# Expert results stored at a row per token and rank instead of added in memory

## The chip, the cores and the metric

The kernel runs on one core of a Trainium2 chip. The metric is the device time of one execution in microseconds, lower is better; a kernel's time is the median of several runs.

## The reference

Two layers over 512 latent tokens and 256 context tokens of 1024 values, float32. A layer is a mixer (attention) and a mixture of experts, each added to the stream through a norm and a gate. The change touches the second half alone:

```python
# moe: t tokens, 64 experts, 8 of them for each token, one shared expert for all
scores = sigmoid(xt @ router_w)
...                                   # idx: the 8 experts of a token, wts: their weights
routed[tok] += (silu(xb @ w1[e]) * (xb @ w3[e])) @ w2[e] * slot_w      # for every block of an expert
shared = (silu(xt @ sw1) * (xt @ sw3)) @ sw2
return routed + shared
# layer: x += gate2 * RMSNorm_post(moe(...))
```

An expert has F = 256 hidden columns, so w1, w3 and w2 are 1 MB each. Layer 0 has 768 tokens, layer 1 has 512 (the context isn't wanted behind it): 6144 and 4096 pairs of token and expert.

## The kernel before

Phases follow each other with a barrier between them. Of a layer they are: `project` and the attention, `settle`, `experts`, `combine`.

`settle` ends the mixer, writes the modulated rows of all tokens to HBM (`h_rows`), routes them, and works out the shared expert, whose result SP stores tile by tile (128 tokens) to `y_rows` (L1060). Vector makes the mask of chosen experts (`r_maskb`, L1324) and a table for each token and expert in bf16: three parts of the weight and two parts of the token's number. GpSimd writes a block of zero rows to both tensors (L1071, L1072). TensorE is at work nearly all through it with the shared expert; the last shared result is taken out of PSUM by L1253.

`experts` runs over blocks of up to 128 tokens of one expert; an expert with more tokens has more blocks, and the last slots of a block can be empty. They point at spare rows behind the last token. Each engine has its own loop over blocks, two blocks a turn, held together by semaphores:

- SP loads w1 and w3 of an expert (two loads of 1024 KB) into one of two halves of `ring`, once Vector has split what was there. ACT issues the load of w2 (1024 KB, L1627).
- Vector makes the one-hot matrix `e_sel` (L1718); TensorE multiplies it with the table (`index`, L1536), which gives each slot's token and weight; Vector puts the token's number into `e_idxs` (L1728), five blocks ahead.
- GpSimd gathers the rows of a block (`gather`, copy L1486 and indirect DMA L1489) and adds a block's results to `y_rows` (`scatter`, copy L1496 and indirect DMA L1501). The order in its loop is gather of block b + 4, scatter of block b. The scatter's first wait is `added`, that the scatter before has landed, since an addition in memory reads its row and writes it later and two experts can have the same token. Both use queue 0.
- TensorE turns the gathered rows (L1545), multiplies them with the split weights (L1559, L1565), turns the gated product (L1574) and multiplies it with w2 (`down`, L1585). ACT casts the weights' high part (L1647) and takes the result out of PSUM times its weight into one of two buffers `e_y` (`rows_out`, L1673, once per block). Vector makes the low part of the weights (`e_w13l`, L1739, four pieces an expert, both inputs in SBUF).

`combine` loads the finished rows of each tile (L1802) and the gate's row for each condition (L1805; two conditions in layer 0, one in layer 1), ACT makes the norm's factor (L1824 to L1826), Vector updates the stream with two instructions a tile (L1849, L1851). In layer 0 ACT goes on to the next norm's sums (L1833 to L1839); in layer 1 SP stores the output (L1810).

```python
def scatter(b, par):
    wait_for(pool, added, 16 * b)
    nc.gpsimd.tensor_copy(sidx[par][:], idxs[:, at_block(b)]).then_inc(s_copied, 1)
    pool.wait_ge(y_ready, b + 1)
    pool.wait_ge(s_copied, b + 1)
    nc.gpsimd.indirect_dma_start(s.yrows[l], ..., ysb[par][:], None, compute_op=ALU.add).then_inc(added, 16)
```

Of the kernel before, what the change touches and what calls it, by code (L numbers as in the profile page):

```python
# [8 lines left out]
F32 = mybir.dt.float32  # L9
F32R = mybir.dt.float32r  # L10
BF16 = mybir.dt.bfloat16
# [6 lines left out]
P = 128  # L18
D = 1024
# [17 lines left out]
ROUTED_SCALE = 2.5  # L37
RING = 3
# [920 lines left out]
def settle(nc, s, a, l, tiles, r):  # L959
# [18 lines left out]
    with ExitStack() as ctx:  # L978
# [22 lines left out]
        maskb = sb("r_maskb", [P, n_t, E], BF16)  # L1001
        wsum, winv = sb("r_wsum", [P, n_t]), sb("r_winv", [P, n_t])
# [23 lines left out]
        zero_ready, ones_ready = sem("zero_ready"), sem("ones_ready")  # L1026
# [15 lines left out]
        def _(sp):  # L1042
# [24 lines left out]
        def _(pool):  # L1067
# [4 lines left out]
            pool.dma_start(s.yrows[l][T:T + P, :], zero[:]).then_inc(zero_out, 16)  # L1072
            pool.wait_ge(zero_out, 32)
# [182 lines left out]
        def _(dve):  # L1256
# [74 lines left out]
            link(nc.vector.tensor_copy(r.tab5[:, :, :, 0], wt[:]))  # L1331
            link(nc.vector.tensor_tensor(res1[:], wt[:], r.tab5[:, :, :, 0], ALU.subtract))
            link(nc.vector.tensor_copy(r.tab5[:, :, :, 1], res1[:]))
            link(nc.vector.tensor_tensor(res1[:], res1[:], r.tab5[:, :, :, 1], ALU.subtract))
            link(nc.vector.tensor_copy(r.tab5[:, :, :, 2], res1[:]))
            for i in range(n_t):
                link(nc.vector.memset(r.tab5[:, i, :, 3], float(i * P - T - P)))
            link(nc.vector.tensor_copy(r.tab5[:, :, :, 4], part[:, 0:1].unsqueeze(2).to_broadcast([P, n_t, E])))
# [60 lines left out]
def experts(nc, s, a, l, n_t, r):  # L1399
# [10 lines left out]
    with ExitStack() as ctx:  # L1410
# [7 lines left out]
        idxs, gws = sb("e_idxs", [P, P], U32), sb("e_gws", [P, P])  # L1418
# [9 lines left out]
        gathered = [sem(f"gathered{i}") for i in range(2)]  # L1428
        (w13_in, w2_in, w13_hi, w13_lo, sel_ready, idx_mm, tok_ready, idx_ready, g_copied, s_copied, xg_clean, xt_mm, x_hi,
         x_lo, h_mm, e_ready, g_ready, gt_mm, gt_ready, y_mm, y_ready, added, pool_clear, sp_clear, act_clear) = (sem(n) for n in (  # L1430
             "w13_in", "w2_in", "w13_hi", "w13_lo", "sel_ready", "idx_mm", "tok_ready", "idx_ready", "g_copied", "s_copied",
             "xg_clean", "xt_mm", "x_hi", "x_lo", "h_mm", "e_ready", "g_ready", "gt_mm", "gt_ready", "y_mm", "y_ready",
             "added", "pool_clear", "sp_clear", "act_clear"))
# [3 lines left out]
        raw2 = s.ring[:, 2, :].rearrange("p (o k n) -> p o k n", o=2, k=KF)  # L1437

# [41 lines left out]
        def _(pool):  # L1480
# [43 lines left out]
            pool.wait_ge(added, 16 * (2 * n + 1))  # L1524
# [4 lines left out]
        def _(pe):  # L1529
            def index(b, par, code):  # L1530
# [4 lines left out]
                for t in range(n_t):  # L1535
                    mm = nc.tensor.matmul(psI[:, 0:5], sel[par][:, t, :], r.tab5[:, t, bass.DynSlice(e, 1), :],  # L1536
# [87 lines left out]
        def _(act):  # L1624
# [50 lines left out]
            def step(b, par, code, later):  # L1675
# [4 lines left out]
                if not isinstance(b, int) or b > 0:  # L1680
                    rows_out(b - 1, 1 - par)
# [13 lines left out]
            step(0, 0, code[0], code[2])  # L1695
            step(1, 1, code[1], code[3])
            with act.Fori(0, n - 1) as i:
                code = codes(act, 2 * i + 2, 4)
                step(2 * i + 2, 0, code[0], code[2])
                step(2 * i + 3, 1, code[1], code[3])  # L1700
# [3 lines left out]
            rows_out(m + 1, 1)  # L1704
            next2(m + 2, code[0])
            gate(m + 2, 0)
            rows_out(m + 2, 0)
# [203 lines left out]
```

## Time and profile before

| | |
|---|---|
| median of 3 runs | 3057.51 us (3044.96 to 3065.29) |
| the profiled execution, and its span | 3069.55 us, 3067.8 us |
| TensorE busy | 87% of the span |
| Vector, ACT, GpSimd busy | 50%, 42%, 18% |
| mean granted clock of TensorE | 0.926 |
| moved by DMA | 645.89 MB |
| blocks of experts, layer 0 and layer 1 | 77 and 71 |
| expert stages, first to last result taken | 720.9 to 1592.9 us, 2226.7 to 3033.3 us |
| addition stages | 1607.6 to 1633.1 us, 3047.7 us to the end |

The span is the profile's own, from the first instruction to the last end; the time around it is some 2 us longer. The profiled execution is 12 us above the median of the three runs. Below, PE is TensorE, DVE is Vector, POOL is GpSimd, L12 is line 12 of the kernel before. Durations and times are in us unless they are marked ns. The expert stages are some 1700 of the 3068 us, the addition stages some 45.

### The profile page before, as it was taken

What the parts mean: (1) busy time and instruction counts of PE and PEld (TensorE: products, weight loads), DVE (VectorE), ACT (ScalarE), POOL (GpSimd) and SP (SyncE); (2) the same over time, 40 slices, a digit from 0 to 9 for tenths busy, and PEclk for the clock granted to TensorE, in tenths of its full rate; (3) what the DMA queues carried; (4) which work ended last, traced back from release to release, by engine and by line L of the source; (5) the groups of instructions that cost most, each with busy time, mean ns of one, the idle gap of its engine ahead of it and who ended that gap; (6) DMA issues with size and microseconds to landing.
All of it is one profiled execution on the core that took longest, in us unless ns stands there. A gap on an engine that the chain in (4) does not pass through costs nothing. (4 is left out here: it accounts for less than half of the span.)

```text
span 3067.8 us, 50203 instructions
## 1 busy us (share of the span) xinstructions
PE 2677.9 (87%) x11125; PEld 1635.2 (53%) x11126; DVE 1534.4 (50%) x2814; ACT 1303.4 (42%) x2063; POOL 561.2 (18%) x624
## 2 busy tenths in 40 slices
PE   5598999978889989999965999989698889989994
PEld 0044454535556666666642444654366666666663
DVE  0143663336555655565634212953555566665562
ACT  1022663215545545454533112642255555555562
POOL 0000000002222332333220000000123323333331
PEclk6699899998999999999987999989899999999997
DMA  9820202128998999798974101011488999999896
GB/s 400 343 74 3 56 1 74 69 97 314 307 292 273 330 313 305 239 323 262 300 194 162 71 11 58 1 41 69 158 296 285 322 311 328 335 319 341 248 328 169
DMA packets 135713, 645.89 MB, mean 211 GB/s; under 512 B 24024, under 2 KB 31192, under 8 KB 78936
## 3 DMA queue, kind: packets, MB, share of 16 engines
q1 hardware_dynamic: 72576, 383.49, 32.9%
q0 software_dynamic: 43200, 121.69, 18.1%
q10 hardware_dynamic: 19864, 139.80, 12.0%
q8 instruction: 39, 0.64, 0.1%
q14 instruction: 34, 0.28, 0.0%
HBM read 588.17 MB, written 92.37 MB: 222 GB/s over the span
## 5 line engine op out<-in xcount | busy, mean ns | idle before, releaser
L1559 PE MATMUL e_psH<-e_w13h,e_xh 128*128 x1184 | 611.6, 517 | 63.6 <-issue 32.3
L1739 DVE TENSOR_TENSOR e_w13l<-ring,e_w13h x512 | 592.7, 1219 | 113.0 <-ACT e_w13h L1647 109.7
L1585 PE MATMUL e_psY<-ring,e_gt 128*128 x1184 | 566.8, 606 | 6.6 <-ACT e_gt L1660 6.6
L1647 ACT CAST e_w13h<-ring x512 | 497.8, 1043 | 163.3 <-DMA ring<-in_exp_w 127.9
L1559 PE MATMUL e_psH<-e_w13l,e_xh 128*128 x1184 | 486.3, 411 | 0.0
L1752 DVE TENSOR_TENSOR e_xl<-e_psT,e_xh 128x512 fp32r<-128x512 f32 x296 | 197.5, 688 | 500.6 <-ACT e_xh L1667 377.5
L1545 PE MATMUL e_psT<-ident,e_xg 128*128 128x128 f32 x1184 | 335.3, 286 | 70.7 <-DMA e_xg<-h_rows,e_gidx 67.6
L459 PE MATMUL psP<-ring,ho 128*128 128x512 f32 x800 | 349.5, 592 | 0.0
L1559 PEld LDWEIGHTS e_psH<-e_w13h,e_xh 128*128 128x128 f32 x1184 | 235.9, 199 | 181.6 <-issue 147.4
L1565 PE MATMUL e_psH<-e_w13h,e_xl 128*128 x1184 | 307.9, 402 | 0.0
L1545 PEld LDWEIGHTS e_psT<-ident,e_xg 128*128 128x128 f32 x1184 | 227.2, 192 | 140.5 <-issue 78.4
L1585 PEld LDWEIGHTS e_psY<-ring,e_gt 128*128 128x128 f32 x1184 | 213.5, 190 | 166.0 <-issue 153.9
L1501 POOL DMA_INDIRECT y_rows<-e_y,e_sidx x148 | 249.0, 1682 | 191.9 <-ACT e_y L1673 89.7
L1667 ACT CAST e_xh<-e_psT 128x512 fp32r<-128x512 f32 x296 | 169.1, 588 | 261.8 <-PE e_psT L1545 156.2
L1559 PEld LDWEIGHTS e_psH<-e_w13l,e_xh 128*128 128x128 f32 x1184 | 237.5, 201 | 18.0 <-issue 17.5
L459 PEld LDWEIGHTS psP<-ring,ho 128*128 128x128 f32 x800 | 149.1, 190 | 173.6 <-issue 173.6
L1565 PEld LDWEIGHTS e_psH<-e_w13h,e_xl 128*128 128x128 f32 x1184 | 211.2, 188 | 43.0
L1496 POOL COPY e_sidx<-e_idxs 128x1 uint32 (+1 forms) x148 | 63.4, 428 | 824.3 <-DMA y_rows<-e_y,e_sidx 824.3
L1673 ACT ACTIVATE e_y<-e_psY,e_gws 128x1024 f32<-128x1024 f32 x148 | 164.1, 1109 | 95.1 <-PE e_psY L1585 73.5
L1489 POOL DMA_INDIRECT e_xg<-h_rows,e_gidx x148 | 166.8, 1127 | 126.5 <-POOL e_gidx L1486 125.6
L1718 DVE TENSOR_TENSOR e_sel<-slots,posm 128x768 bf16 (+1 forms) x156 | 128.9, 828 | 32.5 <-DMA slots<-in_k_slots 30.6
L1486 POOL COPY e_gidx<-e_idxs 128x1 uint32 (+1 forms) x148 | 119.4, 807 | 88.2 <-PE e_psT L1545 65.6
(252 smaller groups left out, 2594.5 us busy)
## 6 DMA issues: line engine op xcount, KB each, us to landing
ring<-in_exp_w SPq DMA_DIRECT2D x256, 1024.0 KB
ring<-in_exp_w ACTq DMA_DIRECT2D x130, 1024.0 KB
ring<-in_ada_w SPq DMA_DIRECT2D x48, 1024.0 KB, 13.3
ring<-in_c_w_in SPq DMA_DIRECT2D x6, 2048.0 KB
ring<-in_sh_w SPq DMA_DIRECT2D x6, 1024.0 KB, 8.6
h_rows<-r_hrow SPq DMA_DIRECT2D x10, 512.0 KB, 2.6
y_rows<-r_y SPq DMA_DIRECT2D x10, 512.0 KB, 2.6
f_Y<-y_rows SPq DMA_DIRECT2D x10, 512.0 KB, 9.4
```

Of the source, the lines that this page charges most:

```text
L459: mm = nc.tensor.matmul(psP[n % 2][:], HT[:, k, t * P:(t + 1) * P], s.ring[:, c % RING, k * 512:(k + 1) * 512], start=(k == 0), stop=(k == ...
L1489: nc.gpsimd.indirect_dma_start(xg[par][:], None, s.hrows[l], bass.IndirectOffsetOnAxis(ap=gidx[par][:, 0:1], axis=0), bounds_check=T, oob_ ...
L1501: nc.gpsimd.indirect_dma_start(s.yrows[l], bass.IndirectOffsetOnAxis(ap=sidx[par][:, 0:1], axis=0), ysb[par][:], None, compute_op=ALU.add) ...
L1545: tr = nc.tensor.transpose(psT[:, k * P:(k + 1) * P], column(xg[par][:], k), s.ident[:])
L1559: nc.tensor.matmul(psH[par][:], xh[par][:, k * P:(k + 1) * P], w[:, bass.DynSlice(half, 1), :, k, :], start=(k == 0 and i == 0), stop=False)
L1565: mm = nc.tensor.matmul(psH[par][:], xl[par][:, k * P:(k + 1) * P], w13h[:, bass.DynSlice(half, 1), :, k, :], start=False, stop=(k == KD - 1))
L1585: mm = nc.tensor.matmul(psY[:, c * 512:(c + 1) * 512], gt[par][:, k * P:(k + 1) * P], raw2[:, bass.DynSlice(half, 1), k, c * 512:(c + 1) * ...
L1647: nc.scalar.copy(w13h[:, bass.DynSlice(half, 1), :, k, :].rearrange("p o u k n -> p (o u) (k n)"), raw13[:, bass.DynSlice(half, 1), :, k, ...
L1667: nc.scalar.copy(xh[par][:, j * 512:(j + 1) * 512], psT[:, j * 512:(j + 1) * 512]).then_inc(x_hi, 1)
L1673: nc.scalar.activation(ysb[par][:], psY[:], ACT.Copy, scale=gws[:, at_block(b)]).then_inc(y_ready, 1)
L1739: nc.vector.tensor_tensor(low, raw, high.bitcast(F32), ALU.subtract).then_inc(w13_lo, 1)
L1752: nc.vector.tensor_tensor(xl[par][:, c], psT[:, c], xh[par][:, c].bitcast(F32), ALU.subtract).then_inc(x_lo, 1)
```

## The change

`y_rows` gets nine rows for each token: one for each rank of its eight experts, and the ninth for the shared expert. An expert's result is stored there, not added, so no store waits for another; each buffer `e_y` has a semaphore of its own (`stored`). Slots of no token get a row number beyond the tensor, and the bounds check of the DMA leaves them out. The rank is the count of chosen experts of lower number: GpSimd sums the mask over the experts in `settle` by six shifted additions, into a sixth column of the table (`tab5` becomes `tab`). In `experts` the index matmul has six columns in place of five, and Vector works out 9 x token + rank with one more instruction on 128x1. The scatter's index copy now comes behind the wait for the result. The zero rows behind `y_rows` are gone.

`combine` loads nine rows a token, 128x9x1024 values a tile, in three DMAs of three rows into one of two buffers. GpSimd adds the middle three (two additions), Vector adds the first three, GpSimd's sum, and the last three (six additions). The next tile's sum comes ahead of the update of the tile before.

```diff
+ROWS = TOPK + 1
...
-                sp.dma_start(s.yrows[l][i * P:(i + 1) * P, :], ysb[i % 2][:]).then_inc(w_out[i % 2], 16)
+                sp.dma_start(s.yrows[l][i * P:(i + 1) * P, TOPK, :], ysb[i % 2][:]).then_inc(w_out[i % 2], 16)
...
-            pool.dma_start(s.yrows[l][T:T + P, :], zero[:]).then_inc(zero_out, 16)
-            pool.wait_ge(zero_out, 32)
+            for i in range(2):
+                nc.gpsimd.memset(below[i][:], 0.0).then_inc(below_step, 1)
+            pool.wait_ge(below_step, 2)
+            pool.wait_ge(mask_ready, 1)
+            lo = E // 2
+            nc.gpsimd.tensor_copy(below[0][:, :, lo + 1:], mask[:, :, 0:E - 1]).then_inc(below_step, 1)
+            for i in range(6):
+                pool.wait_ge(below_step, 3 + i)
+                now = below[i % 2]
+                nc.gpsimd.tensor_tensor(below[1 - i % 2][:, :, lo:], now[:, :, lo:], now[:, :, lo - (1 << i):lo + E - (1 << i)],
+                                        ALU.add).then_inc(below_step, 1)
+            pool.wait_ge(below_step, 9)
+            nc.gpsimd.tensor_copy(r.tab[:, :, :, 5], below[0][:, :, lo:]).then_inc(below_step, 1)
+            pool.wait_ge(zero_out, 16)
...
             def scatter(b, par):
 
-                wait_for(pool, added, 16 * b)
-                pool.sem_inc(pool_clear, 1)
-                nc.gpsimd.tensor_copy(sidx[par][:], idxs[:, at_block(b)]).then_inc(s_copied, 1)
                 pool.wait_ge(y_ready, b + 1)
                 pool.sem_inc(pool_clear, 1)
+                nc.gpsimd.tensor_copy(sidx[par][:], rows[:, at_block(b)]).then_inc(s_copied, 1)
                 pool.wait_ge(s_copied, b + 1)
                 pool.sem_inc(pool_clear, 1)
-                nc.gpsimd.indirect_dma_start(s.yrows[l], bass.IndirectOffsetOnAxis(ap=sidx[par][:, 0:1], axis=0), ysb[par][:], None,
-                                             compute_op=ALU.add).then_inc(added, 16)
+                nc.gpsimd.indirect_dma_start(y_flat, bass.IndirectOffsetOnAxis(ap=sidx[par][:, 0:1], axis=0), ysb[par][:], None,
+                                             bounds_check=ROWS * T - 1, oob_is_err=False).then_inc(stored[par], 16)
...
-            pool.wait_ge(added, 16 * (2 * n + 1))
+            pool.wait_ge(stored[0], 16 * (n + 1))
+            pool.wait_ge(stored[1], 16 * n)
...
-                    mm = nc.tensor.matmul(psI[:, 0:5], sel[par][:, t, :], r.tab5[:, t, bass.DynSlice(e, 1), :],
+                    mm = nc.tensor.matmul(psI[:, 0:6], sel[par][:, t, :], r.tab[:, t, bass.DynSlice(e, 1), :],
...
-            def rows_out(b, par):
+            def rows_out(b, m, par):
 
                 act.wait_ge(y_mm, b + 1)
-                wait_for(act, added, 16 * (b - 1))
+                wait_for(act, stored[par], 16 * m)
                 nc.scalar.activation(ysb[par][:], psY[:], ACT.Copy, scale=gws[:, at_block(b)]).then_inc(y_ready, 1)
...
-                dve.wait_ge(tok_ready, b + 1)
-                nc.vector.tensor_scalar(idxs[:, at_block(b)], tok[:], float(T + P), r.spare[:, 0:1], ALU.add, ALU.min).then_inc(idx_ready, 1)
+                dve.wait_ge(tok_ready, 2 * b + 1)
+                nc.vector.tensor_scalar(idxs[:, at_block(b)], tok[:], float(T + P), r.spare[:, 0:1], ALU.add, ALU.min).then_inc(tok_ready, 1)
+                dve.wait_ge(tok_ready, 2 * b + 2)
+                nc.vector.scalar_tensor_tensor(rows[:, at_block(b)], idxs[:, at_block(b)], float(ROWS), psI[:, 5:6], ALU.mult,
+                                               ALU.add).then_inc(idx_ready, 1)
...
+    THIRD = ROWS // 3
-        Y = sb("f_Y", [P, len(tiles), D])
-        up = sb("f_up", [P, D])
+        Y = [sb(f"f_Y{i}", [P, ROWS, D]) for i in range(2)]
+        side = [sb(f"f_side{i}", [P, D]) for i in range(2)]
+        up = [sb(f"f_up{i}", [P, D]) for i in range(2)]
...
         @block.sync
         def _(sp):
-            for i in range(len(tiles)):
-                sp.dma_start(Y[:, i, :], s.yrows[l][i * P:(i + 1) * P, :]).then_inc(y_in[i], 16)
+            for i in range(n):
+                for g in (1, 0, 2):
+                    if i >= 2:
+                        if g == 1:
+                            sp.wait_ge(side_ready, i - 1)
+                        else:
+                            sp.wait_ge(sum_ready, i - 1)
+                    cols = slice(g * THIRD, (g + 1) * THIRD)
+                    sp.dma_start(Y[i % 2][:, cols, :], s.yrows[l][i * P:(i + 1) * P, cols, :]).then_inc(y_in[i % 2][g], 16)
...
+        @block.gpsimd
+        def _(pool):
+            for i in range(n):
+                y = Y[i % 2]
+                pool.wait_ge(y_in[i % 2][1], 16 * (i // 2 + 1))
+                if i >= 2:
+                    pool.wait_ge(sum_ready, i - 1)
+                nc.gpsimd.tensor_tensor(side[i % 2][:], y[:, THIRD, :], y[:, THIRD + 1, :], ALU.add).then_inc(pool_step, 1)
+                pool.wait_ge(pool_step, i + 1)
+                nc.gpsimd.tensor_tensor(side[i % 2][:], side[i % 2][:], y[:, THIRD + 2, :], ALU.add).then_inc(side_ready, 1)
...
-                act.wait_ge(y_in[i], 16)
-                link(nc.scalar.activation(junk[:], Y[:, i, :], ACT.Square, accum_out=ssq[:, i:i + 1]))
+                act.wait_ge(sum_ready, i + 1)
+                link(nc.scalar.activation(junk[:], up[i % 2][:], ACT.Square, accum_out=ssq[:, i:i + 1]))
...
+            def add_rows(i):
+                y, u = Y[i % 2], up[i % 2][:]
+                if i >= 2:
+                    dve.wait_ge(x_ready, i - 1)
+                dve.wait_ge(y_in[i % 2][0], 16 * (i // 2 + 1))
+                link(nc.vector.tensor_tensor(u, y[:, 0, :], y[:, 1, :], ALU.add))
+                link(nc.vector.tensor_tensor(u, u, y[:, 2, :], ALU.add))
+                dve.wait_ge(side_ready, i + 1)
+                link(nc.vector.tensor_tensor(u, u, side[i % 2][:], ALU.add))
+                dve.wait_ge(y_in[i % 2][2], 16 * (i // 2 + 1))
+                for j in range(2 * THIRD, ROWS - 1):
+                    link(nc.vector.tensor_tensor(u, u, y[:, j, :], ALU.add))
+                nc.vector.tensor_tensor(u, u, y[:, ROWS - 1, :], ALU.add).then_inc(sum_ready, 1)
+
+            def update(i):
+                t, u = tiles[i], up[i % 2][:]
                 dve.wait_ge(rstd_ready, i + 1)
+                link(nc.vector.scalar_tensor_tensor(u, u, rstd[:, i:i + 1], gate[:, 1 if t < CT else 0, :], ALU.mult, ALU.mult))
+                nc.vector.tensor_tensor(s.X[:, t, :], s.X[:, t, :], u, ALU.add).then_inc(x_ready, 1)
+
+            for i in range(n):
+                add_rows(i)
+                if i == 0:
+                    dve.wait_ge(gate_in, 16 * len(conds))
                 if i >= 1:
-                    dve.wait_ge(x_ready, i)
-                nc.vector.scalar_tensor_tensor(up[:], Y[:, i, :], rstd[:, i:i + 1], gate[:, cond, :], ALU.mult, ALU.mult).then_inc(up_ready, 1)
-                dve.wait_ge(up_ready, i + 1)
-                nc.vector.tensor_tensor(s.X[:, t, :], s.X[:, t, :], up[:], ALU.add).then_inc(x_ready, 1)
+                    update(i - 1)
+            update(n - 1)
...
-        s.yrows = [nc.dram_tensor(f"y_rows{l}", [(NTOK if l == 0 else SEQ) + P, D], F32, kind="Internal").ap() for l in range(DEPTH)]
+        s.yrows = [nc.dram_tensor(f"y_rows{l}", [NTOK if l == 0 else SEQ, ROWS, D], F32, kind="Internal").ap() for l in range(DEPTH)]
```

## Rows read from the trace of the kernel before

**Rows 1.** Waits of the whole core: us in total, times, longest.

```profile
POOL e_sidx L1496 <- DMA y_rows<-e_y,e_sidx: 824.3, 145, 9.6
...
PE e_psT L1545 <- DMA e_xg<-h_rows,e_gidx: 67.6, 31, 5.1
...
PE e_psH L1559 <- DVE e_w13l L1739: 25.9, 10, 5.0
```

**Rows 2.** Windows: length; PE, PEld, DVE, ACT, POOL busy; clock, DMA share, GB/s.

```profile
713.90:1587.30 873.40, 808.53 (x3603) 556.71 (x3601) 503.27 (x773) 455.60 (x620) 265.67 (x298) 0.98 0.91 292
2222.20:3027.70 805.50, 746.23 (x3178) 510.55 (x3176) 470.96 (x736) 441.79 (x594) 253.44 (x274) 0.97 0.93 304
```

**Rows 3.** L1673, once a block: each layer, then an undisturbed stretch of each.

```profile
L1673 ACT ACTIVATE e_y<-e_psY,e_gws x77: 1102/1108/1117, 720.9 to 1592.9; 128x1024 f32<-128x1024 f32 x77
...
L1673 ACT ACTIVATE e_y<-e_psY,e_gws x71: 1102/1108/1119, 2226.7 to 3033.3; 128x1024 f32<-128x1024 f32 x71
...
L1673 ACT ACTIVATE e_y<-e_psY,e_gws x17: 1105/1108/1116, 1354.7 to 1525.6; 128x1024 f32<-128x1024 f32 x17
...
L1673 ACT ACTIVATE e_y<-e_psY,e_gws x10: 1107/1109/1114, 2848.3 to 2942.6; 128x1024 f32<-128x1024 f32 x10
```

**Rows 4.** Timeline, layer 0, 1204 to 1217 us: start, duration, idle before.

```profile
1204.33 1.62 POOL L1501 DMA_INDIRECT y_rows<-e_y,e_sidx  x1 [0.81 <-POOL e_sidx L1496]
...
1205.34 4.62 DVE L1739 TENSOR_TENSOR e_w13l<-ring,e_w13h  x4
1205.41 1.19 POOL L1486 COPY e_gidx<-e_idxs 128x1 uint32 x1
...
1215.09 0.18 POOL L1496 COPY e_sidx<-e_idxs 128x1 uint32 x1 [6.49 <-DMA y_rows<-e_y,e_sidx]
...
1216.10 1.62 POOL L1501 DMA_INDIRECT y_rows<-e_y,e_sidx  x1 [0.82 <-POOL e_sidx L1496]
```

**Rows 5.** Queues: packets, MB, share: 700 to 1590; 1594 to 1607; 618.6 to 624.

```profile
q0 software_dynamic: 21464, 63.45, 32.2%
...
q0 software_dynamic: 144, 0.52, 26.2%
...
q1 hardware_dynamic: 144, 0.52, 23.7%
```

**Rows 6.** Window of the first phase, loads of 1024 KB; columns as in rows 2.

```profile
10.00:60.00 50.00, 27.93 (x128) 2.94 (x120) 2.76 (x4) 7.41 (x14) 0.00 (x0) 0.57 1.01 415
```

**Rows 7.** Groups of instructions: count, busy us, mean ns, idle before.

```profile
L1728 DVE TENSOR_SCALAR e_idxs<-e_tok,spare 128x1 f32 (+1 forms) x154 | 32.9, 214 | 7.9
```

**Rows 8.** Two tiles: ns min/median/max, first and last start.

```profile
L708 POOL COPY a_wide<-a_inv x12: 608/610/612, 319.7 to 483.7; 128x512 f32<-128x512 f32 x12
...
L1486 POOL COPY e_gidx<-e_idxs x148: 179/754/1848, 683.2 to 2993.6; 128x1 uint32 x138, 128x1 uint32<-128x1 uint32 x10
```

**Rows 9.** Timeline of `settle` in layer 0: the mask, and the last shared result.

```profile
617.78 0.36 DVE L1324 CAST r_maskb<-r_mask 128x384 bf16<-128x384 f32 x1
...
671.13 1.01 ACT L1253 COPY r_y<-m_psY 128x1024 f32<-128x1024 f32 x1 [3.79 <-PE m_psY L1154]
```

**Rows 10.** Timeline of the addition stages, layer 0 and then layer 1.

```profile
1607.62 0.34 SPq L1802 DMA_DIRECT2D f_Y<-y_rows  x1
...
1611.51 1.06 ACT L1824 ACTIVATE f_junk<-f_Y 128x1024 f32<-128x1024 f32 x1 [2.60 <-DMA f_Y<-y_rows]
...
1628.71 1.28 DVE L1849 SCALAR_TENSOR_TENSOR f_up<-f_Y,f_rstd,f_gate 128x1024 f32<-128x1024 f32 x1 [0.24 <-ACT f_rstd L1826]
...
1630.03 1.22 DVE L1851 TENSOR_TENSOR X<-X,f_up 128x1024 f32<-128x1024 f32 x1
...
1632.86 0.21 ACT L1839 ACTIVATE xrstd<-f_xlog 128x6 f32<-128x6 f32 x1
...
3047.74 0.34 SPq L1802 DMA_DIRECT2D f_Y<-y_rows  x1
...
3063.00 1.22 DVE L1851 TENSOR_TENSOR X<-X,f_up 128x1024 f32<-128x1024 f32 x1
```

More of the change, by code:

```diff
@@ L1001, in settle @@
         maskb = sb("r_maskb", [P, n_t, E], BF16)
+        below = [sb(f"r_below{i}", [P, n_t, E // 2 + E], BF16) for i in range(2)]
         wsum, winv = sb("r_wsum", [P, n_t]), sb("r_winv", [P, n_t])
@@ L1437, in experts @@
         raw2 = s.ring[:, 2, :].rearrange("p (o k n) -> p o k n", o=2, k=KF)
+        y_flat = s.yrows[l].rearrange("t j n -> (t j) n")
         def entry(eng, row, b, top):
@@ L1785, in combine @@
     conds = range(1) if last else range(2)
+    n = len(tiles)
+    THIRD = ROWS // 3
     with ExitStack() as ctx:
@@ L1789, in combine @@
         gate = sb("f_gate", [P, 2, D])
-        Y = sb("f_Y", [P, len(tiles), D])
-        up = sb("f_up", [P, D])
+        Y = [sb(f"f_Y{i}", [P, ROWS, D]) for i in range(2)]
+        side = [sb(f"f_side{i}", [P, D]) for i in range(2)]
+        up = [sb(f"f_up{i}", [P, D]) for i in range(2)]
         junk = sb("f_junk", [P, D])
         ssq, logs, rstd, xss, xlog = (sb(f"f_{n}", [P, NT]) for n in ("ssq", "logs", "rstd", "xss", "xlog"))
-        y_in = [sem(f"y_in{i}") for i in range(len(tiles))]
-        gate_in, act_step, up_ready, rstd_ready, x_ready, out_done = (
-            sem(n) for n in ("gate_in", "act_step", "up_ready", "rstd_ready", "x_ready", "out_done"))
+        y_in = [[sem(f"y_in{i}{g}") for g in range(3)] for i in range(2)]
+        gate_in, act_step, dve_done, pool_step = sem("gate_in"), sem("act_step"), sem("dve_done"), sem("pool_step")
+        side_ready, sum_ready, rstd_ready, x_ready, out_done = (
+            sem(n) for n in ("side_ready", "sum_ready", "rstd_ready", "x_ready", "out_done"))
         block = ctx.enter_context(nc.Block())
@@ L1807, in _ @@
                 out = a["out"].rearrange("o (t p) d -> (o t) p d", p=P)
-                for i in range(len(tiles)):
+                for i in range(n):
                     sp.wait_ge(x_ready, i + 1)
                     sp.dma_start(out[i], s.X[:, tiles[i], :]).then_inc(out_done, 16)
-                sp.wait_ge(out_done, 16 * len(tiles))
+                sp.wait_ge(out_done, 16 * n)
+        @block.gpsimd
[8 more added lines that the diff above has]
+                nc.gpsimd.tensor_tensor(side[i % 2][:], side[i % 2][:], y[:, THIRD + 2, :], ALU.add).then_inc(side_ready, 1)
         @block.scalar
@@ L1828, in _ @@
             nc.scalar.preload_act_table_set(LN_EXP)
-            for i in range(len(tiles)):
+            for i in range(n):
                 statistics(i)
@@ L1834, in _ @@
             if not last:
-                n = len(tiles)
                 act.wait_ge(x_ready, n)
@@ L1842, in _, with link @@
         def _(dve):
-            dve.wait_ge(gate_in, 16 * len(conds))
-            for i, t in enumerate(tiles):
-                cond = 1 if t < CT else 0
-                dve.wait_ge(rstd_ready, i + 1)
+            chain = [0]
+            def link(ins):
+                chain[0] += 1
+                ins.then_inc(dve_done, 1)
+                dve.wait_ge(dve_done, chain[0])
+            def add_rows(i):
[13 more added lines that the diff above has]
+                t, u = tiles[i], up[i % 2][:]
+                dve.wait_ge(rstd_ready, i + 1)
+                link(nc.vector.scalar_tensor_tensor(u, u, rstd[:, i:i + 1], gate[:, 1 if t < CT else 0, :], ALU.mult, ALU.mult))
+                nc.vector.tensor_tensor(s.X[:, t, :], s.X[:, t, :], u, ALU.add).then_inc(x_ready, 1)
+            for i in range(n):
+                add_rows(i)
+                if i == 0:
+                    dve.wait_ge(gate_in, 16 * len(conds))
                 if i >= 1:
-                    dve.wait_ge(x_ready, i)
-                nc.vector.scalar_tensor_tensor(up[:], Y[:, i, :], rstd[:, i:i + 1], gate[:, cond, :], ALU.mult, ALU.mult).then_inc(up_ready, 1)
-                dve.wait_ge(up_ready, i + 1)
-                nc.vector.tensor_tensor(s.X[:, t, :], s.X[:, t, :], up[:], ALU.add).then_inc(x_ready, 1)
+                    update(i - 1)
+            update(n - 1)
 def hybrid_backbone(nc, a, stop=None):
```

42 lines of the change are left out of this document (21 added, 21 removed).

## The prediction

> **What bounds the kernel now.** I read the expert stages first, since both halves of the change touch them. The waits of the whole core [rows 1] name the thing removed: GpSimd stood 824.3 us, in 145 pieces, until the previous scatter-add had landed. That is no gain by itself; what counts is what it makes TensorE wait for. The two stretches of block after block [rows 2] show TensorE busy 808.5 of 873.4 us and 746.2 of 805.5, with the DMA engines busy for 0.91 and 0.93 of the time: both are near full. The starts of the ACT instruction that takes a block's result out of PSUM give the block's period [rows 3]: layer 0 has 77 blocks from 720.9 to 1592.9, 872.0/76 = 11.47 us; layer 1 has 71, 806.6/70 = 11.52 us. Each layer also has an undisturbed run: 17 blocks from 1354.7 to 1525.6 are 10.68 us apart, 10 blocks from 2848.3 to 2942.6 are 10.48. So TensorE's own pace is 10.68 and 10.48, and what the blocks lose over it is 872.0 - 76 x 10.68 = 60 us and 806.6 - 70 x 10.48 = 73 us: 133 us is all that the expert stages can give. Rows 1 say what TensorE waits for there: 67.6 us for gathered rows, 25.9 us for the split weights; after such stops the granted clock is lower for a while (0.98 and 0.97 over the stretches), which makes up much of the rest.
>
> Both waits lead to the DMA engines. A scatter is issued at 1204.33, the next at 1216.10 [rows 4]: 11.8 us, more than the 10.68 TensorE needs, because its index copy waits until 1215.09 for the landing. The gather stands behind the scatter in GpSimd's order, so gathers come late. The engines' time: queue 0 carries scatters and gathers, 32.2% of 890 us = 287 us in layer 0 [rows 5]. Storing 128 rows plainly takes 23.7% of 5.4 us = 1.3 us. The reference routes 768 x 8 = 6144 rows, 48 full blocks, so gathers are about 48 x 1.3 = 61 us, and 77 scatter-adds the other 226, 2.9 us each (the last one, with nothing beside it, 26.2% of 13 us = 3.4). An expert's weights are three loads of 1024 KB, 3.15 MB, 7.6 us at the 415 GB/s of [rows 6]. An expert of one block asks 7.6 + 2.9 + 1.0 = 11.5 us of the engines in a 10.68 us period: it can't keep up. That is the bound of the slow blocks.
>
> **The stores in the expert stages.** A plain store costs 1.3 us for 128 rows, and rows of no token aren't moved: 61 us in place of 226 in layer 0, 41 (4096 rows) in place of 71 x 2.9 = 206 in layer 1. The engines' share falls from 795 to 630 us of about 813 (0.77), and from 749 to 584 of about 732 (0.80); a one-block expert asks 7.6 + 1.0 + 1.0 = 9.6 us, under the period. The chain of landings is gone; GpSimd does copy, store, copy, gather, each issue 1.0 to 1.6 us, some 6 us of a period. The index copy now stands behind the wait for the result: 0.2 us, or up to 1.2 if Vector runs, hidden as nobody needs the store for two blocks. Bounds of the gain: nothing, and all 133 us. I take nine tenths, 120 us, as both causes fall together and the demand is well under the period; a tenth stays for the first blocks, whose weights arrive in a burst.
>
> **Edits at nothing.** The sixth column of the index matmul, and one more Vector instruction on 128x1 with its wait: an instruction of that size takes 0.21 us [rows 7], 148 of them 32 us of Vector, which is busy 503 of 873 us [rows 2]. The rank sums on GpSimd (two fills, two copies, six additions of at most 384 columns, under 1 us each going by 0.61 us for a copy of 512 [rows 8], 10 us together) begin once the mask is there, 617.78, and the stage runs until after 671.13 [rows 9]; without that cover they would cost 20 us in two layers. The zero rows no longer written were hidden in the same place.
>
> **The ends of the stages.** The last result is taken at 1592.9 and the addition stage begins 14.7 us later, at 1607.62 [rows 3, 10]. The last store takes 1.3 in place of 3.4 us of the engines; with its copy no longer waiting for the store before, 2.5 us a layer: -5.
>
> **The addition stage.** Now: 25.4 us in layer 0 (1607.62 to 1633.07), 20.1 in layer 1 (3047.74 to the span's end at 3067.8, of which 3.6 behind the last update, which ends at 3064.2) [rows 10]. Afterwards each tile reads nine rows a token, 4.72 MB, 11.2 us at 415 to 420 GB/s; the gate adds 2.5 us (two conditions) and 1.25. From issue to landing there are 2.6 us beside the data (1607.62 to 1611.51, less 1.3). Vector does six additions of 1.22 us, then 1.28 + 1.22 for the update; with 0.04 between them 7.6 + 2.6 = 10.2 us a tile, alone under 11.2. GpSimd does two additions of 128x1024. No row shows one: the copy of 512 columns in 0.61 us is 1.2 us for one stream of 1024, which is the lower bound; an addition reads two streams, 2.4. I take 2.4, so 4.8 us a tile.
>
> Do they overlap? [rows 4, 8] speak against it: GpSimd's copy of 128x1 takes 0.18 us at best, but the one at 1205.41 took 1.19, as long as the Vector subtraction with two SBUF inputs that had begun at 1205.34. GpSimd reads only once that instruction is over; 0.75 is the median of these copies. I take it to hold in the other direction too, as both read the same inputs' memory: Vector and GpSimd then take turns, 10.2 + 4.8 = 15.0 us a tile, and not the DMA but this pair is the bound.
>
> The Trainium skill (SBUF — State Buffer, Who interferes with whom) says so: a Vector instruction with two SBUF inputs and a GpSimd instruction that reads SBUF exclude each other for a whole instruction, whoever began first. By that rule the sum is the one taken here; the one direction that the trace shows agrees. The Trainium skill (GPSIMD Engine Reference, Elementwise — side-by-side cycle accounting) gives 4.5 us for an addition of 2048 columns; half is 2.25, an estimate from that page, and the sum by it would be 3 us lower. No run here shows it yet.
>
> Layer 0, from the first issue: tile 1's first piece lands at 2.6 + 11.2 + 2.5 + 3.7 = 20.0, GpSimd is through at 24.8, tile 1 is summed at 32.4 and tile 0 updated at 35.0. From there everything has arrived in time and the pair works in turn: GpSimd 4 x 4.8, Vector 4 x 7.6 + 5 x 2.6, to 97.6; statistics 1.9: 99.5, so +74. Layer 1 the same way: 18.8, 23.6, 31.2, 33.8, then 2 x 4.8 + 2 x 7.6 + 3 x 2.6 to 66.4, + 3.6 = 70, so +50. Together +124; with the lower bound for GpSimd +108.
>
> **Sum.** -120 - 5 + 124 = -1 us. The profiled execution took 3069.55 us around its span of 3067.8; the sum gives 3068.5 for it, and 3056 against the median 3057.5.
>
> **The rivals.**
> 1. *Vector and GpSimd overlap.* Then the reads are the bound. Layer 0: 2.6 + 6 x 11.2 + 2.5 = 72.3, three additions 3.8, two updates 5.2, statistics 1.9: 83.2, +58. Layer 1: 48.7 + 3.8 + 5.2 + 3.6 = 61.3, +41. Together +99, the kernel at 3031. For it: the Vector subtractions of rows 4 show no loss (4.62 us for four) beside the 1.19 us copy; against it: that copy itself worked only 0.18 us, so it could hold nobody up.
> 2. *The weights still set the pace: slower.* In the expert stages the loads of w1 and w3 may start only when a half of the ring is free, so the engines can stand idle and then be late; the demand of 9.6 in 10.68 is no proof. If half of the 133 us stays, the gain is 66: 3057.5 - 66 - 5 + 124 = 3110. It decides from a gain under 88 us (3088). For it: 25.9 us of TensorE's waits are for split weights and not for gathers. Against it: in both stretches the engines are at 0.9 or more [rows 2], and the stores relieve them of 165 us a layer, more than all the stops.
> 3. *The reads are slow.* Nine rows lie 36 KB apart per token, in pieces of 12 KB. It shows only under 4.72 MB / 15.0 us = 315 GB/s; at 260 GB/s a tile takes 18.2 us, ten tiles some 30 us more: 3087.
> 4. *All stops go and GpSimd adds at the lower bound.* -133 - 5 + 108: 3027.
>
> **How the numbers follow.** Forecast 0.48 (own range 3038 to 3078), rival 1 0.20, rival 2 0.16, rival 3 0.06, rival 4 0.10. A measurement here tells about 1% (31 us) from no change: faster is under 3027, slower over 3088. Faster: 0.08 of rival 1, 0.06 of rival 4, with larger gains than the sum 0.06 of the forecast's case: 0.20. Slower: 0.13 of rival 2, 0.03 of rival 3, 0.03 of the forecast's case: 0.19. Same 0.61. The range leaves out the lower part of rivals 1 and 4 and most of rival 2: 3020 to 3092.
>
> **What would show it.** In the changed kernel's profile: GpSimd's wait for a landing before the index copy gone; block periods of 10.7 and 10.5 over whole stages, DMA share 0.75 to 0.8, no wait of TensorE for gathered rows; queue 0's share halved or less. In the addition stage: 15.0 us from one tile's last addition to the next, with gaps before Vector's additions as long as GpSimd's, or 11.2 with the DMA at 1.0 if rival 1 holds; GpSimd's addition at 2.4 us. Periods over 11 us, or TensorE waiting for split weights as before, would make it wrong towards slower.

## The result and the profile after

The changed kernel takes 3070.3 us (median of 20 runs), the kernel before 3045.3 us (20 runs beside them): 1.0089 times as long, 95% interval 1.0064 to 1.0115. It is slower by 25 us by the medians and by 27 by the ratio. The ratio is taken over the fast executions alone, without one of the changed kernel that took 4356.8 us at a granted clock of 0.59. The forecast was 3056 us and no change; the time lies inside its range, but the change has a sign, and it is a loss.

The changed kernel's profiled execution took 3077.5 us around a span of 3075.7. Laid beside the one of before (3067.8) the difference of 7.9 us splits up like this:

| stretch | before | after | difference |
|---|---|---|---|
| up to the first result of layer 0 | 720.9 | 719.6 | -1.3 |
| blocks of layer 0, first to last result | 872.0 | 827.5 | -44.5 |
| last result to the first read of the addition stage | 14.7 | 10.8 | -3.9 |
| addition stage, layer 0 | 25.4 | 95.7 | +70.3 |
| from there to the first result of layer 1 | 593.7 | 588.7 | -5.0 |
| blocks of layer 1 | 806.6 | 755.7 | -50.9 |
| last result to first read | 14.4 | 9.4 | -5.0 |
| addition stage, layer 1, to the end | 20.1 | 68.3 | +48.2 |

The waits of the changed kernel (us, times, longest) answer to [rows 1]. GpSimd waits for the result of a block and no more for a landing; TensorE's wait for gathered rows has fallen from 67.6 to 7.2 us, the one for split weights is still there:

```profile
POOL e_sidx L1511 <- ACT e_y L1687: 790.8, 148, 9.3
...
PE e_psH L1573 <- DVE e_w13l L1756: 28.9, 23, 3.2
...
PE e_psT L1559 <- DMA e_xg<-h_rows,e_gidx: 7.2, 2, 4.6
```

The two expert stages in windows (length; PE, PEld, DVE, ACT, POOL busy; clock, DMA share, GB/s), to be held against [rows 2], and the instruction that ends a block, against [rows 3]. The DMA share has gone from 0.91 and 0.93 to 0.79 and 0.81, the granted clock from 0.98 and 0.97 to 0.99. The periods are 827.5/76 = 10.89 us and 755.7/70 = 10.80:

```profile
719.40:1546.90 827.50, 793.27 (x3596) 550.03 (x3596) 511.52 (x840) 453.33 (x616) 217.27 (x296) 0.99 0.79 290
2242.10:2997.80 755.70, 727.76 (x3172) 503.52 (x3172) 477.93 (x796) 438.15 (x590) 205.03 (x272) 0.99 0.81 298
```

```profile
L1687 ACT ACTIVATE e_y<-e_psY,e_gws x77: 1103/1108/1119, 719.6 to 1547.1; 128x1024 f32<-128x1024 f32 x77
...
L1687 ACT ACTIVATE e_y<-e_psY,e_gws x71: 1099/1108/1117, 2242.3 to 2998.0; 128x1024 f32<-128x1024 f32 x71
```

Queue 0 (packets, MB, share of the engines) from 700 to 1540 us moves 48.64 MB in 15.7% of 840 = 132 us of the engines, where [rows 5] have 63.45 MB in 287 us:

```profile
q0 software_dynamic: 21458, 48.64, 15.7%
```

The addition stage of layer 0 in time (start, duration). GpSimd's first addition, with Vector still waiting, takes 2.33 us. Later, where both are at work, each is stretched by the other. Vector's pair of additions from 1600.97 takes 6.52 us in place of 2.49, and GpSimd's addition beside it 3.20. One addition of Vector's that begins inside one of GpSimd's takes 3.25:

```profile
1557.92 1.51 SPq L1830 DMA_DIRECT2D f_Y<-y_rows  x3
...
1564.60 2.33 POOL L1848 TENSOR_TENSOR f_side<-f_Y 128x1024 f32<-128x1024 f32 x1 [14.13 <-DMA f_Y<-y_rows]
...
1572.99 2.49 DVE L1900 TENSOR_TENSOR f_up<-f_up,f_Y 128x1024 f32<-128x1024 f32 x2
...
1600.97 6.52 DVE L1900 TENSOR_TENSOR f_up<-f_up,f_Y 128x1024 f32<-128x1024 f32 x2
...
1603.21 3.20 POOL L1850 TENSOR_TENSOR f_side<-f_side,f_Y 128x1024 f32<-128x1024 f32 x1
...
1615.78 3.25 DVE L1897 TENSOR_TENSOR f_up<-f_up,f_side 128x1024 f32<-128x1024 f32 x1
...
1653.39 0.21 ACT L1877 ACTIVATE xrstd<-f_xlog 128x6 f32<-128x6 f32 x1
```

And that stage's windows. While tiles come in, the DMA engines are full (0.97, 404 GB/s) and Vector is busy 50.5 of 65 us. In the last 27 us Vector is busy throughout, and the transfers end some 7 us into them (no DMA is at work from 1635 on):

```profile
1560.00:1625.00 65.00, 0.00 (x0) 0.00 (x0) 50.48 (x30) 8.89 (x20) 29.83 (x11) 0.50 0.97 404
1625.00:1652.00 27.00, 0.00 (x0) 0.00 (x0) 26.26 (x19) 6.87 (x15) 4.41 (x2) 0.50 0.25 107
```

### The profile page after: what moved, and what is told of

The parts are those of the page before. It is cut to its first block and busy times, and to the rows that moved or that the text cites. A ratio compares the mean times of both kernels' runs of the same rounds, so it can differ in the third digit from the quotient of the medians.

```text
span 3075.7 us, 50783 instructions
## 1 busy us (share of the span) xinstructions
PE 2635.6 (86%) x11125; PEld 1615.8 (53%) x11126; DVE 1668.6 (54%) x3028; ACT 1306.0 (42%) x2063; POOL 534.6 (17%) x662
## 5 line engine op out<-in xcount | busy, mean ns | idle before, releaser
L1573 PE MATMUL e_psH<-e_w13h,e_xh 128*128 x1184 | 596.6, 504 | 66.7 <-issue 30.6
L1573 PE MATMUL e_psH<-e_w13l,e_xh 128*128 x1184 | 476.2, 402 | 0.0
L1559 PE MATMUL e_psT<-ident,e_xg 128*128 128x128 f32 x1184 | 324.7, 277 | 10.5 <-DMA e_xg<-h_rows,e_gidx 7.2
L1573 PEld LDWEIGHTS e_psH<-e_w13h,e_xh 128*128 128x128 f32 x1184 | 229.3, 194 | 184.0 <-issue 147.5
L1559 PEld LDWEIGHTS e_psT<-ident,e_xg 128*128 128x128 f32 x1184 | 225.7, 191 | 63.9 <-DMA e_xg<-h_rows,e_gidx 7.3
L1511 POOL COPY e_sidx<-e_rows 128x1 uint32 (+1 forms) x148 | 104.1, 703 | 790.8 <-ACT e_y L1687 790.8
L1573 PEld LDWEIGHTS e_psH<-e_w13l,e_xh 128*128 128x128 f32 x1184 | 230.8, 195 | 18.0 <-issue 17.5
L1514 POOL DMA_INDIRECT y_rows<-e_y,e_sidx x148 | 152.5, 1030 | 136.1 <-POOL e_sidx L1511 126.3
L1504 POOL DMA_INDIRECT e_xg<-h_rows,e_gidx x148 | 154.2, 1042 | 126.1 <-POOL e_gidx L1501 121.9
L439 PE MATMUL psT<-ident,hrow 128*128 128x128 f32 x96 | 21.6, 398 | 139.5 <-DVE hrow L313 139.5
```

What stands on the lines that cost most here:

```text
L1504: nc.gpsimd.indirect_dma_start(xg[par][:], None, s.hrows[l], bass.IndirectOffsetOnAxis(ap=gidx[par][:, 0:1], axis=0), bounds_check=T, oob_ ...
L1514: nc.gpsimd.indirect_dma_start(y_flat, bass.IndirectOffsetOnAxis(ap=sidx[par][:, 0:1], axis=0), ysb[par][:], None, bounds_check=ROWS * T - ...
L1559: tr = nc.tensor.transpose(psT[:, k * P:(k + 1) * P], column(xg[par][:], k), s.ident[:])
L1573: nc.tensor.matmul(psH[par][:], xh[par][:, k * P:(k + 1) * P], w[:, bass.DynSlice(half, 1), :, k, :], start=(k == 0 and i == 0), stop=False)
```

## The experiments

The question is twofold: what the additions of the new addition stage cost, where the forecast looks right, and why the expert stages gave back less than the 120 us of the forecast. The theory for the second: blocks lost time to what the additions in memory and the empty rows (slots of no token) ask of the DMA engines. The rival: they lost it to the chain, in which each scatter waits for the landing of the one before. Experiments 1, 5, 6 and 7 leave something out and give a wrong result, so layer 1 works on other values; each still has 77 and 71 blocks.

**1. The stores without the sums.** The new expert stages, and an addition stage that reads the shared expert's row alone.

```diff
-                for g in (1, 0, 2):
+                for g in (2,):
-                    cols = slice(g * THIRD, (g + 1) * THIRD)
+                    cols = slice(ROWS - 1, ROWS)
...
+                nc.vector.tensor_copy(u, y[:, ROWS - 1, :]).then_inc(sum_ready, 1)
```

> The new expert stages with an addition stage that reads one row a token (the shared expert's) and adds nothing: it leaves out the sum over the eight ranks. Theory: the two halves add up. The addition stages of the changed kernel cost 118 us over those of before, so this run is 3070 - 116 = 2954 us, 91 under before (ratio 0.970), the expert stages as in the changed kernel (block periods 10.9 and 10.8 us). Rival: the gain was the forecast 120 and something else ate it: 2925 us (0.961).

Measured: 2963.9 us, 0.9732 of before (0.9682 to 0.9782), 82 us under before; a second time 2970.6 us and 0.9760 (0.9718 to 0.9801), 70 us under. The halves add up: 1.0089 - 0.9732 = 0.036, or 109 us for the sums, where the addition stages of the two profiles differ by 112.5. The forecast's 120 and 5 us would have given 0.961, which neither interval holds. In its profile the addition stages take 29.4 and 22.1 us, 6 us more than before, so the expert stages with their ends gave some 88 us. By the ratio of the second time they gave 79.

> The stores alone once more, on the same chip as the two above: 2964 us, 0.973 of before, if the comparison holds from chip to chip.

**2. The chain put back.** The changed kernel, each store behind the landing of the one before.

```diff
             def scatter(b, par):
+                wait_for(pool, added, 16 * b)
                 pool.wait_ge(y_ready, b + 1)
...
-                                             ...).then_inc(stored[par], 16)
+                                             ...).then_inc(added, 16)
```

> The changed kernel, but each store waits again until the one before has landed. Theory: what the change gives in the expert stages comes from the DMA engines' time (an addition takes 2.9 us of them, a plain store 1.3 or less), not from the chain: a plain store is issued and landed well within a period of 10.5 us, so this is within 10 us of the changed kernel, 3060 to 3080. Rival: the chain of landings was the cost: at least half of the 91 us comes back, 3115 us or more.

Measured: 3079.6 us, 1.0098 (1.0067 to 1.0129) beside 1.0089: the chain costs nothing that can be seen. Its waits show that GpSimd does stand at the landing for 408.6 us, and that this does not reach TensorE, which waits 8.0 us for gathers:

```profile
POOL e_sidx L1513 <- DMA y_rows<-e_y,e_sidx: 408.6, 67, 7.4
...
PE e_psT L1560 <- DMA e_xg<-h_rows,e_gidx: 8.0, 2, 4.5
```

**3. Only the empty rows dropped.** The kernel before with one edit. Its result is complete, and its addition stages are those of before.

```diff
-                                             compute_op=ALU.add).then_inc(added, 16)
+                                             bounds_check=T - 1, oob_is_err=False, compute_op=ALU.add).then_inc(added, 16)
```

> The kernel before with one thing changed: rows of no token are left out of the scatter-add by a bounds check. 77 x 128 rows become 6144 in layer 0 and 71 x 128 become 4096 in layer 1: 200 us of the DMA engines' time less of the 330 that the whole change takes from them. Theory, that the engines' time is the cause: six tenths of 91 us, 2990 us (0.982), with the chain of additions in place and the addition stages untouched. Rival, that only the chain matters: within 10 us of before.

Measured: 3012.1 us, 0.9892 (0.9840 to 0.9945); again on another occasion:

> The kernel before without its empty rows once more, as the version that is faster than both: 0.989 of before, 3012 us; within 0.985 to 0.993 if the first comparison was no accident.

Measured again: 3012.2 us, 0.9895 (0.9843 to 0.9947). The gain is 34 us the first time and 28 the second, not the 56 of the theory. Both intervals are clear of no change and of the rival's 10 us, and this version beats the kernel before and the changed one. Queue 0 from 700 to 1560 us: 24.3% of 860 = 209 us of the engines. With the rows of 48 full blocks gathered at 1.3 us, 147 are left for as many added: 3.1 us each, as against the 1.3 of a plain store. The chain is still there (767.3 us), and so are late gathers (39.7 us of TensorE's waits):

```profile
q0 software_dynamic: 21460, 48.66, 24.3%
```

```profile
POOL e_sidx L1496 <- DMA y_rows<-e_y,e_sidx: 767.3, 143, 8.8
...
PE e_psT L1545 <- DMA e_xg<-h_rows,e_gidx: 39.7, 22, 5.0
```

**4. Additions without the chain.** Blocks of even and odd number are added into two tensors, empty rows dropped; no addition waits for the one before it. The second tensor is filled with zeros in `settle`.

```diff
-                wait_for(pool, added, 16 * b)
-                nc.gpsimd.indirect_dma_start(s.yrows[l], ...
+                nc.gpsimd.indirect_dma_start((s.yrows[l], s.zrows[l])[par], ...
...
+                nc.vector.tensor_tensor(Y[:, i, :], Y[:, i, :], Z[:, i, :], ALU.add).then_inc(sum_ready, 1)
```

> Results still added in memory with the rows of no token left out, but blocks of even and odd number into two tensors, so that an addition need not wait for the one before it, only for the one before that (which its buffer waits for anyway); the addition stage reads both and adds them with one more Vector instruction a tile. Theory, that the DMA engines' time is what matters: near the kernel that only drops the empty rows. It spares the late gathers (39.7 us of TensorE's waits in that kernel's profile, of which the stores-only kernels had none) and pays 10 x (1.25 + 1.26) us or less in the addition stages: 3012 - 20 + 15 = 3007 us, 2995 to 3020. Rival, that the chain costs much: 2975 or less, as the expert stages would then be those of the changed kernel (82 us under before) at 15 us for the additions.

Measured: 3024.4 us, 0.9929 (0.9893 to 0.9964), slower than the 2995 to 3020 that were expected and far from the rival's 2975. In its profile the addition stages take 34.5 and 27.1 us, 16 more than before, so the blocks gained 38 us where the chained version gained 34: without the chain, additions cost as much as with it. The late gathers are gone (8.5 us), and TensorE waits for split weights instead, 36.2 us where experiment 3 has 16.9. So one stall took the place of another; what moved it no run shows:

```profile
PE e_psH L1559 <- DVE e_w13l L1739: 36.2, 24, 3.3
```

**5. Stores with the chain, no sums.** Experiment 1 with the edit of 2, so that it differs from experiment 3 by addition against store, by the small edits that go with the new rows (the index column, the place of the index copy), and by its 6 us in the addition stages.

> The stores alone (no sum over the ranks, as in the kernel that measured the expert stages by themselves), each store waiting until the one before has landed. It measures directly what an addition in memory costs over a store with the chain and the missing empty rows the same as in the kernel that only drops the empty rows. Theory: the chain is worth nothing, so within 8 us of the stores alone without a chain, 2956 to 2972, and the step from addition to store is 3012 - 2964 = 48 us. Rival: in the full kernel the chain's cost was hidden by chance; here 2985 or more.

Measured: 2957.6 us, 0.9724 (0.9685 to 0.9763), no worse than without the chain (0.9760 on the same chip). From addition to store: 0.9895 - 0.9724 = 0.017, 52 us, give or take 20 by the two intervals, and 58 with the 6.

**6. The same with empty rows stored.**

```diff
-bounds_check=ROWS * T - 1
+bounds_check=ROWS * (T + P) - 1
-        s.yrows = [... [NTOK if l == 0 else SEQ, ROWS, D] ...
+        s.yrows = [... [(NTOK if l == 0 else SEQ) + P, ROWS, D] ...
```

> The same with the rows of no token stored too, at spare rows behind the others (the sum is left out here as well). The engines get 29 and 39 blocks of rows more, at 1.3 us 38 and 51 us of their time. Theory, that lost time goes with the engines' time: 200 us of it were worth 34 us with additions, so 89 us give 15: 2964 + 15 = 2979. Rival: below the demand at which the engines fall behind, their time costs nothing: within 8 us of the run without empty rows.

Measured: 2966.6 us, 0.9743 (0.9699 to 0.9786), 9 us over experiment 5. The intervals overlap, so no cost can be told; they hold the theory's 15 us as well as the rival's 8 or less, and this experiment alone doesn't decide. Two windows a kernel (columns as above), first experiment 5, then 6: the DMA share rises from 0.80 and 0.83 to 0.84 and 0.90, and TensorE is busy for the same time within 1%:

```profile
720.00:1540.00 820.00, 791.83 (x3596) 549.13 (x3596) 511.82 (x840) 454.96 (x617) 202.86 (x296) 1.00 0.80 293
2200.00:2900.00 700.00, 672.82 (x2963) 466.92 (x2962) 455.93 (x752) 414.76 (x557) 181.57 (x255) 1.00 0.83 305
```

```profile
720.00:1540.00 820.00, 788.95 (x3586) 547.37 (x3585) 507.93 (x833) 451.84 (x614) 200.38 (x295) 1.00 0.84 308
2200.00:2900.00 700.00, 677.57 (x2958) 467.10 (x2957) 455.96 (x748) 416.38 (x558) 189.12 (x258) 0.99 0.90 334
```

Set beside experiment 3 it says more. That kernel adds and drops its empty rows; this one stores and moves them all. Over whole expert stages the share is 0.85 and 0.85 in experiment 3 (below) and 0.84 and 0.88 here, about the same, and yet this kernel is 46 us faster (0.9743 against 0.9895) and its blocks take 825.0 and 757.3 us in place of 847.1 and 765.7. So the share of the DMA engines does not order these kernels; whether rows are added or stored does:

```profile
719.90:1567.00 847.10, 802.88 (x3596) 554.13 (x3594) 498.52 (x764) 451.78 (x617) 266.70 (x295) 0.98 0.85 283
2205.70:2971.40 765.70, 732.52 (x3172) 504.15 (x3172) 467.96 (x727) 439.15 (x591) 247.48 (x271) 0.99 0.85 294
```

By which way an addition holds TensorE up is open: it takes the engines some 3 us and not 1.3, GpSimd's issue of it takes 1.62 us and not 1.03, and TensorE waits longer for gathered rows (39.7 us in experiment 3, 23.3 here, 7.8 in experiment 5). No run changes one of these alone.

**7. Half the weights.** The changed kernel with half the bytes of w1 and w3.

```diff
-                    sp.dma_start(s.ring[:, par, u * KD * F:(u + 1) * KD * F].unsqueeze(1), w[...]...
+                    sp.dma_start(s.ring[:, par, u * KD * F:u * KD * F + KD * F // 2].unsqueeze(1), w[...]...[:, :, 0:KD * F // 2]
```

> The changed kernel, but of w1 and w3 of each expert only half the bytes are loaded (the other half of the ring keeps old values, so the result leaves the right weights out); instructions and waits are the same. It tells what still holds up the blocks, 38 us over the undisturbed pace in the changed kernel's profile. Theory: the weights' transfers; with half of them gone the periods fall to 10.7 and 10.5 us and the kernel to 3070 - 35 = 3035 us. Rival: what is left is the order of ACT's and Vector's work on new weights, not the transfer: periods stay at 10.8 and over, within 10 us of the changed kernel.

Measured: 3075.2 us, 1.0094 (1.0056 to 1.0131), the same as the changed kernel. The theory, 3035 us, fell. The DMA share is 0.63 in both stages, the clock 1.00, and TensorE still waits 43.1 us for split weights (28.9 in the changed kernel):

```profile
730.00:1530.00 800.00, 762.68 (x3482) 530.14 (x3481) 502.12 (x816) 441.84 (x598) 213.24 (x287) 1.00 0.63 213
2250.00:2980.00 730.00, 709.35 (x3134) 492.94 (x3133) 475.62 (x788) 436.62 (x585) 200.66 (x268) 1.00 0.63 217
```

```profile
PE e_psH L1573 <- DVE e_w13l L1756: 43.1, 33, 2.4
```

So fewer bytes of w1 and w3 do not bring the kernel nearer to the undisturbed pace. The pieces differ, though: the periods are 11.01 and 10.67 us where the changed kernel has 10.89 and 10.80. The starts of the first 16 blocks of layer 0 in the changed kernel show where it loses time:

```profile
L1687 ACT ACTIVATE e_y<-e_psY,e_gws x16: 1104/1107/1113, 719.6 to 898.1; 128x1024 f32<-128x1024 f32 x16
```

Fifteen periods at 10.68 are 160 us. The changed kernel takes 18 us more than that, and its later blocks of layer 0 lose nothing. Other profiles with the same expert stages (experiment 1 twice, experiment 8) lose 9 to 17 us in these fifteen and at most 4 later. With half the weights it is 11 us, so no gain can be told there, and the later blocks lose 14. The rival's cause, the order in which ACT and Vector do their work, is what is left for them, but no run took it away: it is argued, not shown.

**8. All additions on Vector.** The changed kernel without GpSimd in the addition stage; SP loads the three parts of a tile in the order in which Vector now adds them.

```diff
-                dve.wait_ge(side_ready, i + 1)
-                link(nc.vector.tensor_tensor(u, u, side[i % 2][:], ALU.add))
+                dve.wait_ge(y_in[i % 2][1], 16 * (i // 2 + 1))
+                for j in range(THIRD, 2 * THIRD):
+                    link(nc.vector.tensor_tensor(u, u, y[:, j, :], ALU.add))
```

> The changed kernel with all eight additions of a tile on Vector and none on GpSimd. Theory: Vector and GpSimd exclude each other, two GpSimd additions of 2.3 us hold Vector up for 4.1 us a tile and save it 2.5: without them a tile takes 8 x 1.26 + 2.6 = 12.7 us in place of 14 to 15, 10 to 15 us less in all, 3057 us, and no addition on Vector over 1.3 us. Rival: Vector's additions of 3.25 us are slow for another reason (the DMA's writes to the same memory): they stay slow, two more a tile cost 25 us or more, 3095 us.

Measured: 3061.8 us, 1.0066 (1.0035 to 1.0097); the interval overlaps with the changed kernel's, but its addition stages in the profile are 88.2 and 63.9 us, 12 less than 95.7 and 68.3. In the profiles, eight additions on one engine are faster than six and two on two. The durations settle why (ns min/median/max); first the changed kernel, then this one:

```profile
L1850 POOL TENSOR_TENSOR f_side<-f_side,f_Y x10: 2337/3200/3208, 1567.0 to 3051.4; 128x1024 f32<-128x1024 f32 x10
L1894 DVE TENSOR_TENSOR f_up<-f_Y x10: 1224/1684/3251, 1568.2 to 3059.5; 128x1024 f32<-128x1024 f32 x10
```

```profile
L1880 DVE TENSOR_TENSOR f_up<-f_Y x10: 1224/1226/1226, 1561.5 to 3040.1; 128x1024 f32<-128x1024 f32 x10
```

The same addition takes up to 3.25 us with GpSimd at work, and never over 1.23 us without, with the same reads going on. So it is GpSimd that holds Vector up here, and the DMA's writes have no part in it.

## Why the prediction was right and wrong

**The sum as a ladder.** Experiments 3, 5 and 1 lead step by step from the kernel before to the changed one. By the ratios, against 3040 to 3046 us: dropping empty rows from the additions -33 us (experiment 3), stores in place of additions -52 (3 to 5), the chain 0 (1 and 5, changed kernel and 2), the sums +109 (changed kernel less 1): +24, where +27 was measured. Each step carries some 15 to 20 us of uncertainty.

**What bounds the kernel now: half right.** The stops of TensorE were read as the DMA engines' want of time. That additions in memory and their empty rows cost the blocks time is so (experiments 3 and 5). That it goes by the engines' share is not: experiments 3 and 6 have about the same share, and the one that stores is 46 us faster. The chain, which stands first in the waits with 824.3 us, is worth nothing that can be seen: experiments 2, 4 and 5 show it from three sides. The text had warned of the size of that wait but then took the chain along as one of two causes that fall together.

**The stores in the expert stages: the step that failed.** 120 us were forecast, nine tenths of the 133 that the blocks lost. The profile gives 95.4 for the same blocks, the medians 88 for stages and ends together (79 the second time). Two errors are in it.
- *What was to be had.* The 133 us were read off one execution of 3069.55 us. The median of 20 runs is 3045.3: that execution was 24 us slower than usual, and its sum was then set against a median as if all kernels shared those 24. The changed kernel's own profiled execution is 7 us over its median. The profiles differ by 8 us, the medians by 25: these 17 us are most of what the sum is off. That the 24 us lay in the blocks is likely but not shown, with one trace of before. The two profiled executions of experiment 1 point that way: the slower is 17.4 us longer, and its blocks alone are 20.9 us longer (831.3 and 767.8 us for 824.9 and 753.3). The front matter had the 12 us between execution and median in view, and the forecast did not use them.
- *What is left.* A tenth, 13 us, was to stay; it was 38 us of the 133 (10.89 and 10.80 against 10.68 and 10.48 us). The first blocks, which were to be the reason, can account for layer 0, where the first 15 periods lose 18 us and the others nothing; that a burst of weights causes it was not tested apart, and halving w1 and w3 left 11 us of it. In layer 1 the first 15 lose 5 us of 22. What holds the others up stays open; it is not the bytes of w1 and w3 (experiment 7).

The parts of the step held: queue 0 asks 132 us for 122 forecast, the DMA shares are 0.79 and 0.81 for 0.77 and 0.80, late gathers are gone.

**Rival 2** (half of the stops stay, gain 66, 3110 us) was as near as the forecast in the block stages: 38 of 133 are left, between its 67 and the forecast's 13. TensorE does wait for split weights as before (28.9 us for 25.9), but that the transfers of the weights set the pace is not borne out by experiment 7.

**The edits at nothing: right.** The six rank additions take 6.73 us from 618.14 on, and all is over at 626.8; the last shared result comes at 670.56, as before at 671.13. The extra Vector instruction takes 0.16 us. The scatter's index copy, behind the result's wait, takes 0.81 us in the median, within the 0.2 to 1.2 of the text, and nobody is seen to wait for it but the store.

**The ends: better than forecast,** -8.9 in place of -5, and 6.3 us at the starts that were not foreseen.

**The addition stages: right.** +118.5 measured for +124, 95.7 us for 99.5 and 68.3 for 70. GpSimd's addition takes 2.33 us alone for an assumed 2.4; Vector and GpSimd do take turns, as read from a copy of 128x1 that took 1.19 us in [rows 4], and rival 1 (+99) falls. The Trainium skill (SBUF — State Buffer, Who interferes with whom) states this exclusion, for either order of beginning; this trace agrees in both directions, 3.25 us for 1.22 on Vector and 3.20 for 2.33 on GpSimd. The sum is a little under the forecast because an addition of GpSimd's costs Vector 2.0 us (3.25 less 1.22) and not the assumed 2.4. Rival 3 falls too: 404 GB/s in the reads. The +108 for GpSimd at its lower bound, which rival 4 uses, comes to +105 by the text's own steps: eight of the ten tiles' pairs stand in them, each 2.4 us shorter.

**The sign, and the luck in the number.** By the medians the stores gained 79 to 88 us and the sums cost 109, so the change loses. The 88 us of rival 2's text is another mark: the gain below which 3057.5 us would grow by 1%. By the forecast's own terms the change loses below a gain of 119 (124 less 5). That 3070 lies inside the range is in part luck. The sum started from a median of 3057.5 us over three runs; from the 3045.3 of 20 runs the same sum gives 3044, 26 us too low. And in the profiles the 25 us that the blocks fell short were offset by 16 elsewhere: the addition stages, the ends and the starts all came out shorter than forecast.

## What to carry to other kernels

A wait at the head of the list need not cost anything. Ask first whether the engine that bounds the kernel waits behind it, and take out that wait alone: here the chain went without any gain, while a bounds check that leaves out rows of no use gave 1.1% where the new layout lost 0.9%. A layout that turns additions in memory into nine stored rows pays with every row it must read back and add: 109 us here, for the 79 to 88 that the stores gave. A high share of the DMA engines names a suspect and not a price: two kernels with about the same share lay 46 us apart. And a gain that is read off one profiled execution holds for that execution: compare it with the median before the sum is made.

## What the runs showed of the hardware

- An addition in memory takes the DMA engines some 3 us for 128 rows of 4 KB, a plain store 1.3, both through the same queue; GpSimd's issue of the DMA takes 1.62 us with the addition (median, [rows 4]) and 1.03 without (mean).
- The share of the DMA engines alone did not tell what they cost. Stores at 0.84 and 0.88 of them (experiment 6, whole expert stages) were 46 us faster than additions at 0.85 and 0.85 (experiment 3), and no more than 9 us slower than stores at 0.80 and 0.81 (experiment 5), which is within the noise.
- With both inputs in SBUF, Vector's addition of 128x1024 takes 1.22 us alone and up to 3.25 beside GpSimd's additions; GpSimd's takes 2.33 alone and 3.20 beside Vector's.
- GpSimd's two copies of 128x1 changed places when the order of the loop changed. The gather's copy fell from a median of 0.75 us [rows 8] to 0.18, and the scatter's rose from 0.18 to 0.81. Whether two engines meet on SBUF is a matter of timing, and shows in the smallest instructions first.
